# Order of the state-space slots: chunk 3 ahead of the transposes of x, z and a low half ahead of x's scaling, C's evacuation ahead of a gate

## What is computed

```
proj = rmsnorm(h) @ w_in               # gives z_a, xs, Bm, Cm, dt_f, dt_b, ...
xbc = silu(depthwise_conv5([xs, Bm, Cm]) + b)
for each direction, forward and backward (32 heads of 64, 8 groups, state 128):
    dt = softplus(dt_raw + bias);  A_cs = cumsum(-exp(A_log) * dt)
    CB = C @ B.T                                   # per group
    Y += (CB * exp(A_cs[l] - A_cs[s]) * tri) @ (x * dt)
y = Y + D_skip * x
out = rmsnorm(y * silu(z_a)) @ w_out
```

## Time and profile before

| | |
|---|---|
| median of 3 runs | 2335.38 us |
| the profiled execution | 2334.73 us |
| its span | 2332.9 us |
| busy in the span: PE, DVE, ACT, POOL | 99%, 77%, 51%, 25% |
| granted clock of PE | 0.998 of full speed |
| slots 1 to 6 on PE | 1077.80 to 1328.72 us |

### The profile page before, as it was taken

How to read it: one execution, slowest core, us unless ns; L and a number is a source line. 1 busy time by engine, 2 the same in 40 slices (tenths; PEclk the granted TensorE clock), 3 DMA queues, 4 the chain that set the end, 5 groups by cost and what they waited for, 6 DMA issues and landing times.

```text
span 2332.9 us, 51145 instructions
## 1 busy us (share of the span) xinstructions
PE 2311.9 (99%) x17404; PEld 2192.8 (94%) x17404; DVE 1801.6 (77%) x3189; ACT 1198.6 (51%) x1735; POOL 583.8 (25%) x421
## 2 busy tenths in 40 slices
PE   9999999999999999999999999999999999999997
PEld 9999888888888888899999999999999999999997
DVE  7777888888888766689888889989873566666666
ACT  5444455555555444457666743343544444444444
POOL 0230000000000000013423368888788211111100
PEclk9999999999999999999999999999999999999999
DMA  8544656666665666655555545555555554555444
GB/s 312 187 166 145 200 199 209 207 204 205 202 209 201 211 197 195 193 186 194 178 187 173 189 169 180 180 180 198 175 180 180 191 174 164 169 169 180 160 164 152
DMA packets 152908, 438.19 MB, mean 188 GB/s; under 512 B 32387, under 2 KB 47148, under 8 KB 152700
## 3 DMA queue, kind: packets, MB, share of 16 engines
q1 hardware_dynamic: 149276, 424.42, 53.7%
q0 software_dynamic: 3264, 12.41, 2.0%
q10 hardware_dynamic: 288, 0.30, 0.0%
HBM read 434.88 MB, written 11.09 MB: 191 GB/s over the span
## 4 chain that ended last, share of the span: by engine, by line
PE 85%; DVE 8%; issue 3%; ACT 3%; DVEq 1%; DMA 0%; ACTq 0%; SPq 0%
PE bank L1194 24%; PE bank L1177 15%; PE bank L1179 14%; PE bank L1178 14%; PE bank L1195 12%; DVE wlo L1657 2%; DVE c L2084 1%; ACT whi L680 1%; DVE bank L2310 1%; PE bank L1440 1%; PE bank L1560 1%; PE bank L1550 1%; PE bank L1540 1%; PE bank L1567 0%; ACT L663 0%
## 5 line engine op out<-in xcount | busy, mean ns | idle before, releaser
L680 ACT CAST whi<-raw 128x1024 fp32r<-128x1024 f32 x784 | 817.2, 1048 | 508.1 <-PE bank L1179 359.1
L1657 DVE TENSOR_TENSOR wlo<-raw,whi 128x1024 fp32r<-128x1024 f32 x624 | 761.8, 1226 | 224.7 <-ACT whi L680 210.9
L1177 PE MATMUL bank<-xhl,whi 128*128 128x272 f32 (+1 forms) x3024 | 859.3, 284 | 1.2 <-DVE nvt L2456 0.4
L1179 PE MATMUL bank<-xhl,wlo 128*128 128x272 f32 (+1 forms) x3024 | 848.9, 281 | 0.0
L1178 PE MATMUL bank<-xhl,whi 128*128 128x272 f32 (+1 forms) x3024 | 848.6, 281 | 0.0
L1177 PEld LDWEIGHTS bank<-xhl,whi 128*128 128x128 f32 x3024 | 567.7, 188 | 5.1 <-issue 2.2
L1178 PEld LDWEIGHTS bank<-xhl,whi 128*128 128x128 f32 x3024 | 567.8, 188 | 0.6 <-issue 0.2
L1179 PEld LDWEIGHTS bank<-xhl,wlo 128*128 128x128 f32 x3024 | 567.6, 188 | 0.0
L1194 PE MATMUL bank<-xhl,whi 128*128 128x512 f32 x1408 | 469.9, 382 | 0.3 <-DVE ug L1987 0.3
L618 POOL TENSOR_TENSOR wlo<-raw,whi 128x1024 fp32r<-128x1024 f32 x160 | 381.5, 2392 | 94.9 <-ACT whi L680 94.8
L1195 PE MATMUL bank<-xhl,wlo 128*128 128x256 f32 x1408 | 384.4, 273 | 0.0
(11 more groups left out here) (292 smaller groups left out, 2781.4 us busy)
## 6 DMA issues: line engine op xcount, KB each, us to landing
raw<-w_up SPq DMA_DIRECT2D x176, 512.0 KB, 4.3
raw<-w_na SPq DMA_DIRECT2D x128, 512.0 KB, 3.6
raw<-w_ssm SPq DMA_DIRECT2D x96, 512.0 KB, 3.7
raw<-w_glu SPq DMA_DIRECT2D x96, 512.0 KB, 3.6
raw<-w_down SPq DMA_DIRECT2D x80, 512.0 KB, 3.7
raw<-w_qkv SPq DMA_DIRECT2D x48, 512.0 KB, 3.7
raw<-w_mix SPq DMA_DIRECT2D x32, 512.0 KB, 3.7
raw<-w_outa SPq DMA_DIRECT2D x32, 512.0 KB, 3.6
```

The source lines that it names most:

```text
L680: A.copy(whi[s][:, :], raw[s][:, :]).then_inc(sem("hi_done"), 1)
L1177: T.matmul(to_, wh, xh_, start=head, stop=False)
L1179: ins = T.matmul(to_, wl, xh_, start=False, stop=last)
L1657: V.tensor_tensor(wlo[s][:, :], raw[s][:, :], whi[s][:, :].bitcast(F32), SUB).then_inc(sem("lo_done"), 1)
```

## The change

On PE a slot that isn't the last runs chunk 3 ahead of the transposes of x (the first slot did so already). On DVE the middle slots 1 to 6 evacuate z's second tile and make the low half `low(S, 4)` ahead of `turned`; `low(S, 4)` stood between `weights(S, 2)` and `weights(S, 3)`. Later in the same slots, `evac_x(S, 1)`, which takes C off its bank, goes ahead of `gated(S, 1)`.

```
@@ PE: slot
                 chunk_(2)
+                if not end:
+                    chunk_(3)
                 if begin:
-                    chunk_(3)
                     pe.wait_ge(sem("dtr_ready"), 1)
                 turning(S)
-                if not begin:
+                if end:
                     chunk_(3)
@@ DVE: slot
                     low(S, 3)
+                    if not end:
+                        evac_z(S, 1)
+                        low(S, 4)
                     turned(S)
-                    evac_z(S, 1)
+                    if end:
+                        evac_z(S, 1)
                 weights(S, 2)
-                if not end and not begin:
-                    low(S, 4)
                 weights(S, 3)
...
                     gated(S, 0)
                     low_y(S, 0)
+                    evac_x(S, 1)
                     gated(S, 1)
-                    evac_x(S, 1)
                     taps_x(S, 1)
                     low(S, 8)
```

## The result

The changed kernel takes 2338.90 us (median of 19 runs, 2337.22 to 2340.99), the kernel before 2335.38 (19 runs, 2333.19 to 2337.56). The ratio is 1.0016, with a 95% interval of 1.001 to 1.0023: a small loss of 3.5 us, sure in its sign. The prediction was +1.04 us, 2336.4, with a range up to 2338.9, and it took for granted that nothing under about 0.2% could be told from no change; the 19 runs of each kernel tell 0.16%. The sign was right, the size is a bit over three times mine and at the very end of the range.

The account below looks back on a forecast made before the run. PE, 99% busy, was taken to bound the kernel, with DVE and ACT pacing slots 2 to 4. Slot growths of 0.38 + 0.22 = 0.60, then 0.82, then 1.04 gave 2335.38 + 1.04 = 2336.4 us, range 2333.2 to 2338.9.

Parts of the forecast that it names:

- the loop: State-space slots: C's taps, SiLU of C, ACT's run, cast, DVE's run; claimed longer than PE's 41.22 us in slots 2 to 4.
- Chunk 3 ahead of the transposes: the wait goes, the time stays: PE, slot 1: the 1.9 us wait at the transposes goes; the 2.13 us won is lost waiting for C at the similarity.
- Cost of low(4) ahead of the scaling: +1.11 us: DVE, slots 1 to 6: low(4) idles some 1.4 us for ACT's cast, costing +1.11 us a slot.
- C's move gives back 0.73 in slot 1 and 0.89 in the others: DVE: gated(1) fills the idling between C's evacuation and its taps, gaining 0.73 us in slot 1, 0.89 in others.
- +0.22 instead of the +1.11: DVE, slot 3: with gated(1) over before C's taps, they come only 0.22 us later, not 1.11.
- the +0.38 of slot 1: DVE, slot 1: C's taps start at 1116.49 instead of 1116.11, +0.38 us, after low(4)'s cost and C's move.
- rival B: POOL's clamps lengthen C's taps by 0.26 us more in slots 1 to 4: 2337.5 us, or 2335.4 if saved; chance 0.12.
- In slots 5 and 6 PE's own 41.22 us set the pace: Slots 5 and 6: PE, not DVE and ACT, sets the time, so they add 0 and carry the 1.04 us to the end.

Follow-up runs that it names:

- kernel 1: Only PE's part of the change (chunk 3 ahead of the transposes) on the kernel before, DVE's list as before; ratio 0.9996, 2333.55 us.
- 4: The changed kernel with low(4) moved behind the scaling of x, z's second tile still evacuated ahead of it; ratio 0.999 to the kernel before.
- 5: The changed kernel with ACT's cast for low(4) moved ahead of the SiLU of z's second tile, slots 1 to 6; ratio 0.9988 to the kernel before.
- 8: The changed kernel with DVE's loop over slots 2 to 5 written out, same work; ratio 0.9998 to the kernel before.
- 9: POOL's clamps for groups 1 to 7 replaced by constant fills, on the kernel before and the changed one (output not right); single times 2335.96 and 2335.15 us.

## Where the prediction held and which step failed

DVE's run, from the start of the slot's first low half to the end of C's taps, is read from each timeline, as done above for slot 3, and cut at B's and C's taps (us):

| slot, kernel | run | to B's taps | B's taps | to C's taps | C's taps |
|---|---|---|---|---|---|
| 1, before | 27.98 | 17.74 | 2.21 | 5.55 | 2.47 |
| 1, after | 28.63 | 18.85 | 2.58 | 4.59 | 2.62 |
| 3, before | 29.55 | 18.07 | 2.69 | 5.92 | 2.87 |
| 3, after | 30.18 | 19.18 | 3.08 | 5.12 | 2.81 |
| 5, before | 28.91 | 18.08 | 2.43 | 5.79 | 2.61 |
| 5, PE's part alone | 29.55 | 18.08 | 2.65 | 5.93 | 2.88 |
| 5, after | 30.17 | 19.17 | 3.08 | 5.11 | 2.81 |
| 1, before, fills | 27.27 | 17.76 | 2.11 | 5.30 | 2.11 |
| 1, after, fills | 27.65 | 18.85 | 2.11 | 4.59 | 2.11 |
| 2, before, fills | 29.12 | 18.09 | 2.78 | 5.81 | 2.44 |
| 2, after, fills | 29.55 | 19.19 | 2.79 | 5.13 | 2.44 |
| 3, before, fills | 28.98 | 18.08 | 2.43 | 6.03 | 2.44 |
| 3, after, fills | 29.17 | 19.18 | 2.43 | 5.12 | 2.43 |

The rest of the loop, from the end of C's taps through ACT's run to the next low half, is 12.15 us from slot 3 to slot 4 of the kernel before (1202.19 to 1214.35) and 12.08 in the changed one (1204.32 to 1216.39). So the loop exceeds PE's 41.25 when DVE's run is over 29.1 to 29.2 us. Slot 5 of kernel 1 is a test of it: 29.55 + 12.15 = 41.70, and its window is 41.73. For the changed kernel's slot 5 it gives 30.17 + 12.08 = 42.25, and the window is 42.25. Window 1 is apart, since PE comes to slot 1 ahead of the loop.

*Chunk 3 ahead of the transposes: the wait goes, the time stays.* Right. Kernel 1 shows it alone. On the changed kernel PE came to the similarity 2.1 us before C was there and stood for it (longest wait 2.1): all that the transposes had given.

*Cost of low(4) ahead of the scaling: +1.11 us.* Right to the digit: 17.74 to 18.85 in slot 1, 18.07 to 19.18 in slot 3. Kernels 4 and 5 remove the cause from two sides.

*C's move gives back 0.73 in slot 1 and 0.89 in the others.* Right in slot 1: with fills the net of both edits is 27.65 - 27.27 = 0.38, as predicted. In the looped slots it gives back 0.21 less. DVE idles 0.32 us between C's evacuation and gated(1) there, so gated(1) ends behind ACT's first tap and not before it: C's taps start 1.65 us behind the evacuation, and the prediction kept the 1.44 of before. With fills slot 2 shows it alone, 29.55 - 29.12 = 0.43 us, that is 0.22 + 0.21. (The 2.78 of B's taps in that slot stands in both kernels: one step between two taps is 0.35 us longer there, and no tap is. Slot 3's 29.17 - 28.98 = 0.19 looks like the predicted 0.22 by chance: in the kernel before with fills DVE comes to C's bank ahead of PE there and waits, which lengthens the run that is subtracted by some 0.2.) Written out, the slots start C's taps 1.37 us behind the evacuation.

*The step that failed: "+0.22 instead of the +1.11", the loop's growth in each looped slot, and the +0.38 of slot 1, both with the taps' lengths left as they were.* Measured, the growth was 0.65 in slot 1 and 0.62 in slot 3. Slot 3's is 0.22, plus the 0.21 of idling above, plus 0.2 net from POOL's clamps: B's taps +0.39 (3.08 for 2.69), C's -0.06, and two short instructions between them -0.13 together. In slot 1 all of the 0.27 over the forecast goes with the clamps: B's taps took 2.58 for 2.21, C's 2.62 for 2.47, and between them 0.23 was saved. I had put this as rival B, at C's taps and 0.26 a slot; it fell mostly on B's taps. They came 1.1 us later, while the clamps start after PE's outputs: in slot 3 B's taps began 0.62 us ahead of the first clamp before the change, and 0.43 behind it after. The fills prove that the lengths are POOL's doing.

The Trainium skill, page "SBUF — State Buffer", section "SBUF: two separate sides", says that a DVE instruction with two SBUF inputs excludes only a POOL instruction that reads SBUF; the fills, which read nothing, leave the taps at 0.50 us, and so this trace agrees. Its harder half, that the loser waits for the whole instruction, doesn't come out for a tap. Here are B's second tap and the clamp beside it in slot 3 of the kernel before:

```profile
1191.35 0.76 DVE L2084 SCALAR_TENSOR_TENSOR c<-pad,vec,c 128x272 f32<-128x272 f32 x1
1191.33 1.18 POOL L579 TENSOR_SCALAR ef<-bc,acsr 128x272 f32<-128x272 f32 x1 [26.76 <-PE bank L1440]
```

The tap started inside the clamp, took 0.26 us more than its 0.50, and ended 0.4 us ahead of the clamp's end. The ends of spans on POOL are rough, so this is as far as the rows go.

*The second failure: "In slots 5 and 6 PE's own 41.22 us set the pace".* Right for 6 (a written-out slot, run 28.5 us), wrong for 5. In the execution before DVE's run was 28.91 there, in kernel 1, with the same list on DVE, 29.55, of which 0.49 is in the two groups of taps. Slot 5 belongs with 2 to 4; after the change it is 42.25. That is 1.03 us, the largest single error. The trace of before could have warned me: slot 5's run plus 12.15 is 41.06, a margin of 0.19, so a growth of 0.22 already uses it up. But that alone would have given 0.03 us; the run grew by 1.26: 0.43 by the order, as in slot 2 with fills, and 0.65 and 0.20 in the two groups of taps, which the clamps had mostly spared in that one execution of the kernel before. Why they had isn't shown.

*Not foreseen at all:* slot 7's outputs wait 0.4 us for the scaling of x. DVE comes to the last slot later with respect to PE.

The sum in its terms, as changes of windows 1 to 6: predicted -0.01, +0.61, +0.22, +0.22, 0 and 0, together 1.04; measured +0.29, +0.61, +0.56, +0.42, +1.03, -0.03, then slot 7's 0.4 to 0.5: 3.3 us, against 3.5 between the medians. The match of window 2 (+0.61 twice) is luck: the measured one holds growths that were both mis-sized, with a part of slot 1's already spent in window 1.

## What to carry to other kernels

A wait on the fullest engine is a symptom: find the loop of engines that delivers what it waits for, add up that loop, and compare it with the fullest engine's own period. Here PE's wait of 1.9 us at one place simply moved to the next consumer, and moving one cast and one tap on another engine took both nearly away. When a low half or a cast is moved ahead, look at what must be finished on the other engine between: place something long (here the scaling, 1.86 us) over it. And a window that looks undisturbed may have a margin of 0.2 us only; slots that run the same list should be priced alike. Below the full engine's pace a growth of the loop costs nothing, above it every tenth counts: that is why each of four unlike edits (4, 5, 8 and 9) took away nearly all that the loop had cost in windows 2 to 6.

## What the runs showed of the hardware

- A tap of 128 x 272 with two SBUF inputs on DVE takes 0.50 us alone and up to 0.91 beside POOL's clamps; beside POOL fills it stays at 0.50. POOL pays too: its busy time in window 1 rose from 19.86 to 22.26 us. The low half, which also has two SBUF inputs, hardly paid: in slot 1 of the changed kernel one took 1.21 us, as elsewhere, inside a clamp of 2.49, where the clamp shown above took 1.18.
- In a loop with registers, linked DVE instructions start 0.65 us apart, written out 0.53, for the same 0.50 us of work: about 0.12 us for each linked instruction, some 1.3 us over a slot's twelve such steps between taps.
- After its own evacuation DVE took 0.32 us to start gated(1) in the looped slots and under 0.05 in the written-out ones.
